# Expert weights in chunks of 4096 columns in four slots, up matmuls 512 columns wide

## The reference, cut to what matters

```
D_MODEL, SEQ, D_FF, N_EXPERTS, TOP_K = 1024, 256, 2816, 8, 2
logits = einsum('nd,de->ne', xt, router_w)          # 256 x 8
top_val, top_idx = top_k(logits, 2)
gates = softmax(top_val)
# for each expert e, on the tokens xb that chose it:
y = (silu(xb @ w1[e]) * (xb @ w3[e])) @ w2[e]       # w1, w3: 1024 x 2816, w2: 2816 x 1024
out[token] += gate * y
```

## Time and profile before

| | us |
|---|---|
| median of three runs (2298.0 to 2301.26) | 2299.86 |
| the profiled execution, its own time | 2297.79 |
| its span, first to last instruction | 2295.7 |
| PE busy | 2079.4 |
| DVE busy | 1383.6 |
| ACT busy | 836.4 |

### The profile page before, as it was taken

How to read it: one execution, slowest core, us unless ns; L and a number is a source line. 1 busy time by engine, 2 the same in 40 slices (tenths; PEclk the granted TensorE clock), 3 DMA queues, 4 the chain that set the end, 5 groups by cost and what they waited for, 6 DMA issues and landing times.

```text
span 2295.7 us, 28944 instructions
## 1 busy us (share of the span) xinstructions
PE 2079.4 (91%) x12163; PEld 1848.5 (81%) x12163; DVE 1383.6 (60%) x1655; ACT 836.4 (36%) x960; POOL 32.8 (1%) x74
## 2 busy tenths in 40 slices
PE   4987999699999896779999878999999999999987
PEld 4877888478787764579887768998989899998966
DVE  6788867431552213387631126878888787878852
ACT  2411111211153102111011115766667676766641
POOL 2000000000000000000000000000000000000000
PEclk7998999799999997789999987999999999999998
DMA  9746212233332341045663106998999898999960
GB/s 297 257 128 219 71 61 80 83 134 110 110 101 83 112 141 42 19 129 183 185 191 129 64 27 252 351 331 330 351 341 342 325 359 317 335 352 333 346 238 19
DMA packets 225573, 452.13 MB, mean 197 GB/s; under 512 B 6928, under 2 KB 91160, under 8 KB 225448
## 3 DMA queue, kind: packets, MB, share of 16 engines
q1 hardware_dynamic: 222128, 445.44, 55.2%
q0 software_dynamic: 1632, 4.75, 0.7%
q10 hardware_dynamic: 1688, 0.15, 0.1%
HBM read 448.21 MB, written 2.10 MB: 196 GB/s over the span
## 4 chain that ended last, share of the span: by engine, by line
PE 87%; DVE 8%; ACT 2%; issue 1%; DMA 0%; ACTq 0%; DVEq 0%; POOL 0%
PE bank L853 22%; PE bank L1623 18%; PE bank L879 11%; PE bank L1827 9%; PE bank L548 8%; PE bank L629 2%; PE bank L824 1%; PE bank L1659 1%; PE bank L831 1%; DVE arena L2524 1%; PE bank L864 1%; PE bank L1653 1%; DVE arena L2525 1%; PE bank L1686 1%; PE bank L679 1%
## 5 line engine op out<-in xcount | busy, mean ns | idle before, releaser
L1462 DVE TENSOR_TENSOR ring_r<-ring,his_r 128x2816 fp32r<-128x2816 f32 (+1 forms) x192 | 587.0, 3087 | 56.9 <-ACT his_r L1093 56.6
L1093 ACT ACTIVATE his_r<-ring 128x2816 fp32r<-128x2816 f32 (+1 forms) x192 | 491.2, 2561 | 196.9 <-DMA ring<-in_moe_w_dram 184.9
L853 PE MATMUL bank<-his_r,hg_r 128*128 128x352 f32 x2048 | 355.5, 325 | 0.8 <-ACT hg_r L1104 0.8
L853 PEld LDWEIGHTS bank<-his_r,hg_r 128*128 128x128 f32 x2048 | 332.9, 188 | 2.0 <-issue 0.9
L1623 PE MATMUL bank<-hT,ring 128*128 128x256 f32 x1168 | 268.2, 392 | 21.3 <-DVE hT L2350 9.9
L1623 PEld LDWEIGHTS bank<-hT,ring 128*128 128x128 f32 x1168 | 228.9, 197 | 59.8 <-issue 24.0
L1827 PE MATMUL bank<-hT,ring 128*128 128x256 f32 x912 | 214.6, 392 | 14.4 <-DVE arena L2370 10.7
L1827 PEld LDWEIGHTS bank<-hT,ring 128*128 128x128 f32 x912 | 174.6, 195 | 42.5 <-issue 18.2
L853 PE MATMUL bank<-ring_r,hg_r 128*128 128x352 f32 x1024 | 186.1, 324 | 0.0
L853 PEld LDWEIGHTS bank<-ring_r,hg_r 128*128 128x128 f32 x1024 | 169.2, 188 | 0.0
L1623 PE MATMUL bank<-arena,ring 128*128 128x256 f32 x672 | 153.8, 386 | 16.8 <-DVE arena L1317 9.7
(11 more groups left out here) (442 smaller groups left out, 2333.2 us busy)
## 6 DMA issues: line engine op xcount, KB each, us to landing
ring<-in_moe_w_dram SPq DMA_DIRECT2D x128, 1408.0 KB, 8.3
ring<-in_moe_w_dram SPq DMA_DIRECT2D x48, 1536.0 KB, 9.2
ring<-in_even_w_in_dram SPq DMA_DIRECT2D x28, 1024.0 KB, 6.5
ring<-in_ada_w_dram SPq DMA_DIRECT2D x24, 1024.0 KB, 8.6
ring<-in_ffn_w_dram SPq DMA_DIRECT2D x22, 1024.0 KB, 5.3
ring<-in_odd_w_in_dram SPq DMA_DIRECT2D x9, 2048.0 KB, 7.7
ring<-in_moe_w_dram SPq DMA_DIRECT2D x16, 1024.0 KB, 6.9
ring<-in_a_w_in_dram SPq DMA_DIRECT2D x6, 2048.0 KB, 7.9
```

What stands on the lines that cost most here:

```text
L853: ins = mm(bank[first + m][:, 0:WC], x[:, KT // 2 * late + k, :], w[:, k, WC * m:WC * m + WC], start=(not late and k == 0 and s == "hg_hi" ...
L1093: A(moe_hi(n), moe_w(n), ACT.Copy).then_inc(sem("moe_hi"), 1)
L1462: V.tensor_tensor(moe_lo(n), moe_w(n), moe_hi(n).bitcast(F32), ALU.subtract).then_inc(sem("moe_lo"), 1)
```

## The change

The up weights are cut in three groups of 1024, 1024 and 768 columns (GROUPS holds half of each, the width of one matmul: 512, 512, 384) in place of four of 704. An expert has 12 up chunks, of 4096 columns (2048 KB) for the first 8 and 3072 (1536 KB) for the last 4, and 6 down chunks of 4 row tiles (4096 columns, 2048 KB), the last of 2: 18 chunks in place of 24. The ring has four slots of 4096 columns, the high parts three places. HALVES lists the column ranges of AA that the six blocks of an expert fill. The turns and the select move to other chunks, and the select from chunk 10 of 24 to chunk 8 of 18. The overflow rounds use three slots (ORING) in place of four.

```diff
-WC = 352
-MRING = 5
-MSLOT = 3072
-HSLOTS = 4
+GROUPS = (512, 512, 384)
+MRING = 4
+MSLOT = 4096
+HSLOTS = 3
+ORING = 3
...
-        W2F = [3, 3, 3, 3, 3, 3, 2, 2]
+        W2F = [4, 4, 4, 4, 4, 2]
...
-        UPS, DOWNS = 2 * FF // WC, len(W2F)
+        UPS, DOWNS = 4 * len(GROUPS), len(W2F)
...
-            return (KT // 2, 2 * WC) if j < UPS else (W2F[j - UPS], D)
+            return (KT // 2, 2 * GROUPS[j // 4]) if j < UPS else (W2F[j - UPS], D)
...
-                k0, c0 = KT // 2 * (j % 2), 2 * WC * (j // 4)
-                v = (up1, up3)[j // 2 % 2][ex, :, k0:k0 + KT // 2, c0:c0 + 2 * WC]
+                k0, c0, wide = KT // 2 * (j % 2), 2 * sum(GROUPS[:j // 4]), 2 * GROUPS[j // 4]
+                v = (up1, up3)[j // 2 % 2][ex, :, k0:k0 + KT // 2, c0:c0 + wide]
...
+        HALVES = [slice(2 * sum(GROUPS[:c]) + m * GROUPS[c], 2 * sum(GROUPS[:c]) + (m + 1) * GROUPS[c])
+                  for c in range(len(GROUPS)) for m in range(2)]
...
-        TURNS = {5: (0,), 9: (1,), 13: (2, 3), UPS: (4, 5)}
-        GSEL_AT, SCAT_AT, GATHER_AT, SELECT_AT = 3, 1, UPS + 3, 10
+        TURNS = {5: (0,), 6: (1,), 9: (2,), 10: (3,), UPS: (4, 5)}
+        GSEL_AT, SCAT_AT, GATHER_AT, SELECT_AT = 3, 1, UPS + 2, 8
...
-                            ins = mm(bank[first + m][:, 0:WC], x[:, KT // 2 * late + k, :], w[:, k, WC * m:WC * m + WC],
+                            ins = mm(bank[first + m][:, 0:wide], x[:, KT // 2 * late + k, :], w[:, k, wide * m:wide * m + wide],
...
-                pe.wait_ge(sem("moe_gated"), (UPS // 2) * e + 2 * -(-min(512 * g + 512, FF) // (2 * WC)))
+                pe.wait_ge(sem("moe_gated"), (UPS // 2) * e + sum(h.start < min(512 * g + 512, FF) for h in HALVES))
...
-                    pe.wait_ge(sem("moe_silu"), (UPS // 2) * e + 8)
+                    pe.wait_ge(sem("moe_silu"), (UPS // 2) * (e + 1))
...
-                            A(AA[:, WC * p:WC * p + WC], bank[2 * (e % 2) + m][:, 0:WC], ACT.Silu).then_inc(sem("moe_silu"), 1)
+                            A(AA[:, HALVES[p]], bank[2 * (e % 2) + m][:, 0:GROUPS[p // 2]], ACT.Silu).then_inc(sem("moe_silu"), 1)
...
-                            aa = AA[:, WC * p:WC * p + WC]
-                            V.tensor_tensor(aa, aa, bank[2 * ((e + 1) % 2) + m][:, 0:WC], ALU.mult).then_inc(sem("moe_gated"), 1)
+                            aa = AA[:, HALVES[p]]
+                            V.tensor_tensor(aa, aa, bank[2 * ((e + 1) % 2) + m][:, 0:GROUPS[p // 2]], ALU.mult).then_inc(sem("moe_gated"), 1)
```

More of the change, by code:

```diff
@@ L446, in build @@
         OVER = reg(15472, 4)
-        OSLOT = [reg(15480 + 3072 * s, 3072) for s in range(RING)]
+        OSLOT = [reg(15480 + MSLOT * s, MSLOT) for s in range(ORING)]
         OVERI = sb("overi", [1, 4], I32)
@@ L486, in finish_sync @@
                     for j in range(UPS + DOWNS):
-                        if j >= RING:
-                            sp.wait_ge(sem("moe_acc"), PER * (r + NE) + j - RING + 1)
+                        if j >= ORING:
+                            sp.wait_ge(sem("moe_acc"), PER * (r + NE) + j - ORING + 1)
                         k, n_ = moe_shape(j)
-                        sp.dma_start(OSLOT[j % RING][:, 0:k * n_].rearrange("p (k n) -> p k n", k=k), moe_src(j, e))\
-                            .then_inc(sem(f"loaded_{j % RING}"), 16)
+                        sp.dma_start(OSLOT[j % ORING][:, 0:k * n_].rearrange("p (k n) -> p k n", k=k), moe_src(j, e))\
+                            .then_inc(sem(f"loaded_{j % ORING}"), 16)
             sp.wait_ge(sem("toks_taken"), TK_OUT + 4)
@@ L844, in up @@
                         pe.wait_ge(sem("moe_gated"), (UPS // 2) * e)
-                first = 2 * ((gate + e) % 2)
+                first, wide = 2 * ((gate + e) % 2), GROUPS[c]
                 w_lo, w_hi = moe_tiles(moe_lo(n), n), moe_tiles(moe_hi(n), n)
@@ L916, in weights @@
                 def weights(j):
-                    pe.wait_ge(sem(f"loaded_{j % RING}"), 16 * (loads[j % RING] + j // RING + 1) + 16 * (PER // RING) * r)
+                    pe.wait_ge(sem(f"loaded_{j % ORING}"), 16 * (loads[j % ORING] + j // ORING + 1) + 16 * (PER // ORING) * r)
                     k, n_ = moe_shape(j)
-                    return OSLOT[j % RING][:, 0:k * n_].rearrange("p (k n) -> p k n", k=k)
+                    return OSLOT[j % ORING][:, 0:k * n_].rearrange("p (k n) -> p k n", k=k)
                 gather(sem("psel_ready"), 4 * (r + NE) + 2, sem("gather_ready"))
@@ L933, in over_expert @@
                         for k in range(KT // 2):
-                            ins = mm(bank[2 * gate + m][:, 0:WC], HG[:, KT // 2 * late + k, :], w[:, k, WC * m:WC * m + WC],
+                            ins = mm(bank[2 * gate + m][:, 0:GROUPS[c]], HG[:, KT // 2 * late + k, :],
+                                     w[:, k, GROUPS[c] * m:GROUPS[c] * m + GROUPS[c]],
                                      start=(not late and k == 0), stop=(late == 1 and k == KT // 2 - 1))
@@ L1138, in over @@
                     act.wait_ge(sem("moe_acc"), PER * (r + NE) + (4 * (p // 2) + 2))
-                    A(AA[:, WC * p:WC * p + WC], bank[p % 2][:, 0:WC], ACT.Silu).then_inc(sem("moe_silu"), 1)
+                    A(AA[:, HALVES[p]], bank[p % 2][:, 0:GROUPS[p // 2]], ACT.Silu).then_inc(sem("moe_silu"), 1)
                 for g in range(6):
@@ L1524, in over @@
                     dve.wait_ge(sem("moe_silu"), (UPS // 2) * (r + NE) + (p + 1))
-                    aa = AA[:, WC * p:WC * p + WC]
-                    V.tensor_tensor(aa, aa, bank[2 + p % 2][:, 0:WC], ALU.mult).then_inc(sem("moe_gated"), 1)
+                    aa = AA[:, HALVES[p]]
+                    V.tensor_tensor(aa, aa, bank[2 + p % 2][:, 0:GROUPS[p // 2]], ALU.mult).then_inc(sem("moe_gated"), 1)
                 for g in range(4):
```

## The result

Over 20 runs each the changed kernel takes 2305.41 us (2299.9 to 2309.3) against 2299.84 us before (2297.4 to 2302.6): ratio 1.0021, 95% interval [1.0014, 1.0028]. The forecast was 2308; it lost 5.6 us where 8 were expected. The profiled execution took 2305.78 us (span 2304.0) against 2297.79 before.

What follows compares the result with a forecast made beforehand. PE's order of work was taken to bound the kernel, with DMA waiting for slots. Wider matmuls -2.4 us and eight stalls at chunk 12 +11.6 give +9.2 us on 2297.79 (2299.86 median): forecast 2308 us, range 2296 to 2320.

Steps and rivals of the forecast that it cites:

- What binds: Expert stretch: PE busy throughout while DMA has pauses, so PE's order of work sets the time, 102.42 us an expert.
- Matmuls: Up matmuls on PE: fewer, wider ones with the same columns save 0.30 us an expert, 2.4 us over eight.
- ACT and DVE: Splitting chunks into high and low parts: about 1 us less fixed cost on each engine, off the path, worth 0.
- The one tight place: Chunk 12, first of the down weights: its load must land within 7.75 us of issue, or PE stalls once.
- The landing: Chunk 12's load: 7.7 us plus 1.5 for the load before, 9.2 us; late by 1.45, 11.6 over eight experts.
- Ends: Before and after the experts: PE's start stays behind the router, pg1 waits for hT, not weights; 0 us.
- The sum: Whole kernel: -2.4 + 11.6 = +9.2 us, giving 2307.0 from the profiled execution, 2309.1 from the median; forecast 2308.
- A: Rival: chunk 12's load lands in time, so not slower; 2295.4 to 2302 us, 2297 in the middle; chance 0.31.
- B: Rival: each matmul has a hidden fixed cost, so fewer are clearly faster; 14 us less, 2284; chance 0.05.
- C: Rival: coarser chunks make PE late at several places an expert; 25 us slower, 2323; chance 0.12.
- The clock: PE's clock around the stalls: costed at nothing; if it fell, every 20 us at half speed would cost 10.

Runs made afterwards that it cites:

- small group first: Changed kernel with up groups of 384, 512, 512 columns in place of 512, 512, 384, turns moved to suit: 2294.93 us, ratio 0.9982 to the kernel before.
- second profile: Changed kernel run again, unaltered, and profiled again: 2304.68 us, ratio 1.0021 to the kernel before; profiled execution 2301.75 us.
- select later: Changed kernel with the next expert's select moved from chunk 8 to chunk 10: 2315.57 us, ratio 1.0075 to the kernel before.
- smaller down chunks: Changed kernel with down chunks of 3, 3, 4, 4, 4, 4 row tiles: 2303.58 us; with ACT's turn copy before the next high part as well: 2302.92 us.
- four slots: Kernel before with four ring slots of 3072 columns in place of five, nothing else: 2340.88 us, ratio 1.0174.
- cut in two: Changed kernel with every up matmul split into two of half the width (256 and 192 columns): 2332.5 us, ratio 1.0143 to the kernel before.
- the copy first: Changed kernel with ACT copying turned products before the next chunk's high part, not behind it: 2295.55 us, ratio 0.9986 to the kernel before.

## Why the prediction was right

- **What binds.** PE's order of work, with DMA not short: right. Where the window was lengthened (small group first), DMA fed PE through all eight experts with a single stall, of 0.35 us.
- **Matmuls.** Forecast -2.4 us, measured -2.6 in the changed kernel (809.6 without stalls against 812.3). Widths of 512 and 384 took 233.1 ns (48 in 11.19 us) and 174.8 ns (48 in 8.39 us, in the chain of the small group first), forecast 233.1 and 175.8.
- **ACT and DVE.** Forecast 3.64 and 4.42 us for 4096 columns, measured 3.63 and 4.42.
- **The one tight place.** Chunk 12, its third part, released by DVE behind ACT behind DMA, once in each of the eight experts and nowhere else: right, with a limit of 7.75 us against 7.73 in most experts.
- **The landing.** Forecast 9.2 us, measured 8.7 to 9.6, 9.1 on average, and 8.4 to 9.4, 8.9 on average, in the second profile. The forecast was 7.7 us for the bare transfer and 1.5 for the load ahead of it. Bare, with the load before it landed, 2048 KB took 7.6 to 9.2 us, 7.9 on average (21 loads of the two profiles), which leaves 1.0 to 1.2 for the load ahead. The 1.5 had been taken over unscaled from smaller loads closer together, and that the two errors cancel in part is luck. The term was 8 x 1.45 = 11.6 us, measured 11.1 in one profile and 9.5 in the other. By the Trainium skill (DMA: Bandwidth & Descriptors, section Anatomy of one DMA — SWDGE), whose fit is for loads issued by GpSimd while these are issued by SP, the load would have landed at an estimated 6.8 us and nothing been lost; the trace does not agree, with 7.6 us as the fastest bare one.
- **Ends.** Costed at nothing, and equal in the first pair of profiles; but the tail takes one of two lengths some 3.7 us apart, by the clock at pg1's start, and the start of the experts differs by up to 5 us between profiles (1404.0 to 1409.3).
- **The sum.** Forecast +9.2 us, +8.0 in the first pair of profiles, +5.6 in medians. The profiled execution of before was 2.1 us under the median of its runs, that of the changed kernel 0.4 us over its own; that is the difference between +8.0 and +5.6. Against the forecast, stalls give 0.5 to 2.1 us less and the matmuls 0.2 us less. The remainder is within what the ends move by themselves. Seven of the changed kernel's twenty runs lie at 2299.9 to 2302.6 us and thirteen at 2305.2 or over; that the seven had the short tail is my reading, and one profile, at 2301.75 us, shows it.
- **The rivals.** A (it lands in time) never came about in 16 landings, of which the fastest took 8.4 us. B: 2.9 ns an extra matmul, no hidden cost at 256 columns and over. C: no second tight place; chunk 13 and the next expert's chunk 1 were in time.
- **The clock** was costed at nothing, rightly for stalls of up to 1.7 us; where it fell after stalls of 2.15 us and more (select later), it added 1.5 to 1.7 us to each.
- Of what I expected of the experiments, four sizes failed. Two by the same fault, the queue of loads: a chunk issued close behind two others lands at 9.7 us on average and up to 10.8 (smaller down chunks), and with one slot less many places are tight at once (four slots). One left out the clock (select later), one the floor under narrow matmuls (cut in two).

## What to carry to other kernels

Where chunk sizes in a ring are mixed, check every large chunk whose load runs while small ones are worked: issue to need against landing plus everything queued ahead of it on each engine. Two short instructions in the wrong place of an in-order queue (1.2 us) turned a gain of 0.1% into a loss of 0.2%. Put large chunks before large ones, or small work ahead of the wait for a load; then a coarser grain keeps what it saves.

## What the runs showed of the hardware beyond that

- Up matmuls, each with a weight load of its own, were spaced 111.3 ns at 192 columns, where the line through 256 to 512 columns gives 89.9: a floor, seen at this width alone. The 118 ns at 256 columns is close above it.
- After long stretches at full clock, PE's stalls of up to 2.0 us were never followed by matmuls at the lower clock (16 of 16 in the two profiles of the changed kernel). Of the longer ones, those of 2.15 to 2.6 us with the select later were, four of four; with four slots two were (2.3 us each) and two were not (2.2 and 2.4 us). The length of the stall alone does not decide it.
- A load of 2048 KB took 7.6 to 9.2 us, 7.9 on average, when the one before had landed; issued 4.2 us after one of 1536 KB it took 8.1 to 9.7, 8.9 on average (32 loads of four profiles: the changed kernel's two, the copy first and the select later); issued behind two of 1536 KB, 8.2 to 10.8, 9.7 on average (16 loads of two profiles).
